# Two transformer blocks on one core: the norms between the layers taken tile by tile, and their scale vectors moved into the weights

## The chip, the cores and the metric

The kernel runs on one core of a Trainium2 chip. The metric is the device time of one execution in microseconds (us); lower is better. TensorE (PE) does the matrix products, VectorE (DVE), ScalarE (ACT) and GpSimd (POOL) the rest, and SyncE (SP) starts most of the loads. Each engine works through a queue of its own in order; engines are tied by semaphores.

## The reference, cut to what matters

Two blocks run over 512 tokens of width 1024, in float32. The part that matters here lies between the first block's mixer and the second block's input projection:

```
mix = concat(attention, gmlp) @ w_out                       # [512, 1024]
h   = h + rms_norm(mix, norm_mix_post)
t   = rms_norm(h, norm_ffn_pre)
ffn = (silu(t @ w_gate) * (t @ w_up)) @ w_down              # inner width 2816
h   = h + rms_norm(ffn, norm_ffn_post)
proj = rms_norm(h, attn_norm_2) @ w_in_2                    # [512, 2048], start of block 2
rms_norm(x, g) = x * rsqrt(mean(x*x) + 1e-6) * g
```

So behind each of the products with w_out and w_down there are two norms in a row: one of the product, whose result is added to the residual, and one of the sum, which feeds the next product. Block 2 goes on with attention, a pooling mixer, routing over 32 experts, and the experts; none of that is touched.

## The kernel before, in words

Tokens lie in four tiles of 128. X holds the residual, four tiles of [128, 1024]. XP is the input of a projection, transposed (features on partitions, 8 feature tiles by 512 tokens), as a high and a low part; each product is made of three matmuls, high by high, high by low, low by high (pe_mm3, lines 225 to 228).

The weights come in chunks of at most 4 feature tiles by 512 columns (front_chunks, line 58; w_out is chunks 14 to 17, w_gate_up 18 to 39 in 11 pairs, w_down 40 to 51, w_in_2 52 to 59). SP loads them, by a list in order, into three ring slots (sp_load). ScalarE copies a loaded chunk into WH (act_split, line 214) and VectorE makes the remainder WL (dve_split, line 222). There are three slots of WH and WL, so the split of one chunk waits for the end of the product three splits before (semaphore p_pr), and the product waits for w_lo. A split's number is four below its chunk's number here: split 13 is chunk 17. A chunk of w_out, w_down or w_in_2 has four outputs, one for each token tile, in PSUM banks 0 to 3 (H0) or 4 to 7 (H1); a chunk of w_gate_up has four outputs of 128 features by 512 tokens.

Behind w_out and behind w_down stands the same pair of norms. act_post squares the eight outputs (line 351) and, once X is updated, X's four tiles (line 357). dve_post adds the sums (line 361), has POOL take the power -0.5 of all four columns (line 282), and then for each tile and half scales the product out of PSUM (line 373) and adds it to X (line 376). When all four tiles are there, the mean (line 277), the power and four diagonal tiles (line 287) are made, and pe_rms_T multiplies X by the diagonals, which scales and transposes at once (line 300; a float32 matmul leaves two records). act_put and dve_put (lines 310 and 317) scale by norm_ffn_pre or attn_norm_2 on the way from PSUM into XP. Both vectors lie transposed in GT, columns 8 to 15 and 16 to 23.

The ffn runs in eleven steps f of 256 gate and 256 up columns: two splits, then silu on ScalarE (line 1107) and the product with up on VectorE (line 1129), which writes HIDT. For w_down, HIDT is copied and split four feature tiles at a time, into two buffers in turn (HID2, lines 1085 and 1091); the last block has two tiles. The first copy waits for all of f = 10. The order on each engine is written out by hand in act_wout, dve_wout, act_ffn, dve_ffn, act_mix2 and dve_mix2. act_mix2 issues eleven loads on ScalarE's queue (lines 1204 to 1208) and then small steps for the rotary tables, which VectorE shares (lines 1271 to 1300).

Of the kernel before, what the change touches and what calls it, by code (L numbers as in the profile page):

```python
# [7 lines left out]
F32 = mybir.dt.float32  # L8
# [16 lines left out]
H0, H1 = (0, 1, 2, 3), (4, 5, 6, 7)  # L25

# [20 lines left out]
class Chunk:  # L47
# [4 lines left out]
    def __init__(self, src, k0, nk, cols, nout, raw=False):  # L52
        self.src, self.k0, self.nk, self.cols = src, k0, nk, cols
        self.w = sum(w for _, w in cols)
        self.nout, self.raw = nout, raw


def front_chunks():
# [3 lines left out]
    def columns(src, cols, nout, nk=8):  # L62
        for k0 in range(0, nk, 4):
            out.append(Chunk(src, k0, 4, cols, nout))

    def both(src, nk):
        for k0 in range(0, nk, 4):
            for half in range(2):
                out.append(Chunk(src, k0, min(4, nk - k0), [(512 * half, 512)], 4))
# [9 lines left out]
    both("w_out", 8)  # L79
# [5 lines left out]
    both("w_out_2", 8)  # L85
# [25 lines left out]
def program(nc, A):  # L111
    ctx = ExitStack()
    with ctx:
# [46 lines left out]
        SSN = SMALL[:, 28:32]  # L160
        XP = (RA[:, 0:4096].rearrange("p (k n) -> p k n", k=8), RA[:, 4096:8192].rearrange("p (k n) -> p k n", k=8))
        HID2 = [tuple(RA[:, 4096 * z + 2048 * c:4096 * z + 2048 * c + 2048].rearrange("p (k n) -> p k n", k=4) for c in range(2))
# [43 lines left out]
        def act_split(e, j):  # L206
# [7 lines left out]
            e.activation(WH[:, j % 3, 0:n], RING[:, ch.slot, 0:n], ACT.Copy).then_inc(s("w_hi"), 1)  # L214

        def dve_split(e, j):
            if j not in SPLIT:
# [4 lines left out]
            e.tensor_tensor(WL[:, j % 3, 0:n], RING[:, ch.slot, 0:n], WH[:, j % 3, 0:n].bitcast(F32), ALU.subtract  # L222
                            ).then_inc(s("w_lo"), 1)
# [45 lines left out]
        POW = {"mix": 1, "gln": 2, "post1": 3, "ffn": 4, "post2": 5, "mix2": 6, "moe": 7, "emb": 11, "gate": 12}  # L269
        XT = {"mix": 0, "mid": 8, "ffn": 16, "mix2": 24, "qk": 32, "mid2": 40, "emb": 48, "gate": 50}  # L270
        DG = {"mix": 1, "ffn": 2, "mix2": 3, "gate": 4}
# [72 lines left out]
        def act_post(e, p, c, JUNK, junk2):  # L344
            for half in range(2):
                for i in range(4):
                    n = 8 * p + 4 * half + i
                    e.wait_ge(s("p_pr"), CH[c[half]].first_out + i + 1)
                    if n:
                        e.wait_ge(s("a_sp"), n)  # L350
                    e.activation(JUNK[:, 0:512], PS[(H0, H1)[half][i]][:, :], ACT.Square,
                                 accum_out=SSP[:, 4 * half + i:4 * half + i + 1]).then_inc(s("a_sp"), 1)
            for i in range(4):
                e.wait_ge(s("v_x"), 8 * p + 2 * i + 2)
                if i >= 2:
                    e.wait_ge(s("a_ss"), 4 * (p + 1) + i - 1)
                e.activation(junk2[i % 2], X[:, i, :], ACT.Square, accum_out=SSN[:, i:i + 1]).then_inc(s("a_ss"), 1)

        def dve_post(e, p, stage, GROW, JUNK, row):
            e.wait_ge(s("a_sp"), 8 * p + 8)  # L360
            e.tensor_tensor(SS4, SSP[:, 0:4], SSP[:, 4:8], ALU.add).then_inc(v_c.sem, v_c.up())
            e.wait_ge(v_c.sem, v_c.n)
            dve_mean(e, stage, SS4, 1.0 / 1024, EPS)
            e.wait_ge(s("g_r4"), POW[stage])
            e.wait_ge(s("d_row"), row)
            for i in range(4):
                for half in range(2):
                    b = (H0, H1)[half][i]
# [2141 lines left out]
```

## Time and profile before

| | us |
|---|---|
| median of 3 runs (2344.99 to 2345.92) | 2345.06 |
| the profiled execution's own time | 2344.97 |
| its span | 2343.0 |
| TensorE busy | 2144.6 (92%) |
| VectorE busy | 1542.5 (66%) |
| ScalarE busy | 1338.4 (57%) |
| GpSimd busy | 263.2 (11%) |

The span is the stretch between the first and the last recorded instruction; the execution's own time has about 2 us around it. A busy engine is one with an instruction running; PEclk is the clock that was granted to TensorE, 1.00 for 2.4 GHz and 0.50 for 1.2 GHz. Durations of matmuls contain the way through the array, so the cost of one in a stream is the distance from start to start.

### The profile page before, as it was taken

Reading aid. Unit: us, or ns where it says so; the run is one execution under the profiler, and the core shown is the slowest. Engines: PE = TensorE matmul, PEld = TensorE weight load, DVE = VectorE, ACT = ScalarE, POOL = GpSimd, SP = SyncE. Lnnn points to the kernel's source line nnn. Section 1 sums busy time; section 2 is a strip of 40 time slices with the busy share of each in tenths; the row PEclk is TensorE's granted clock in tenths of the full one; section 3 lists DMA queues with packets and bytes.
Section 4 is the critical chain, followed back from the end, with each engine's and each line's share of the span. In section 5 each row is a group of like instructions: output and inputs, shape, how many; then the busy total and the mean of one; then the engine's idle time right before and its main releaser. Section 6 shows DMA issues by size and latency. Waiting matters only on the chain.

```text
span 2343.0 us, 31680 instructions
## 1 busy us (share of the span) xinstructions
PE 2144.6 (92%) x10622; PEld 1769.4 (76%) x10622; DVE 1542.5 (66%) x1777; ACT 1338.4 (57%) x1690; POOL 263.2 (11%) x254
## 2 busy tenths in 40 slices
PE   3985798699989879886999999999999999999999
PEld 3874687588868767665788888888888888888877
DVE  3214782422223245657898898898988988988884
ACT  3212452312222233423788888888888888888874
POOL 0000000000000000002221221211222212212220
PEclk9987699799999989798999999999999999999999
DMA  3332001122322312032899999999999999999971
GB/s 136 95 125 80 1 2 63 50 103 90 106 74 81 116 65 95 1 115 82 329 366 372 359 369 362 364 364 360 373 365 361 374 358 373 357 361 367 370 278 66
DMA packets 87455, 511.25 MB, mean 218 GB/s; under 512 B 17286, under 2 KB 19930, under 8 KB 29787
## 3 DMA queue, kind: packets, MB, share of 16 engines
q1 hardware_dynamic: 70304, 484.46, 55.1%
q0 software_dynamic: 9536, 16.81, 2.9%
q10 hardware_dynamic: 7546, 9.06, 1.2%
q8 instruction: 45, 0.74, 0.1%
q14 instruction: 24, 0.19, 0.0%
HBM read 503.44 MB, written 23.07 MB: 225 GB/s over the span
## 4 chain that ended last, share of the span: by engine, by line
PE 88%; DVE 6%; ACT 2%; issue 2%; DMA 2%; ACTq 1%; POOL 0%; POOLq 0%; DVEq 0%; SPq 0%
PE PS L1995 15%; PE PS L1997 15%; PE PS L1996 15%; PE PS L226 10%; PE PS L227 10%; PE PS L228 10%; PE PS L1992 2%; PE PS L907 1%; PE PS L300 1%; PE PS L1885 1%; PE PS L2005 1%; DMA RING<-c_oh 1%; PE PS L975 1%; PE PS L1335 1%; PE PS L552 1%
## 5 line engine op out<-in xcount | busy, mean ns | idle before, releaser
L1879 DVE TENSOR_TENSOR WL<-RING,WH 128x2048 fp32r<-128x2048 f32 x388 | 879.6, 2287 | 95.3 <-ACT WH L1875 92.0
L1875 ACT ACTIVATE WH<-RING 128x1024 fp32r<-128x1024 f32 x776 | 811.7, 1059 | 200.2 <-PE PS L1997 176.9
L1995 PE MATMUL PS<-WH,RA 128*128 128x512 f32 x1540 | 639.5, 415 | 0.0
L1997 PE MATMUL PS<-WH,RA 128*128 128x512 f32 x1540 | 600.9, 390 | 0.0
L1996 PE MATMUL PS<-WL,RA 128*128 128x512 f32 x1540 | 600.4, 390 | 0.0
L222 DVE TENSOR_TENSOR WL<-RING,WH 128x2048 fp32r<-128x2048 f32 (+2 forms) x60 | 133.5, 2224 | 482.4 <-ACT WH L214 482.4
L214 ACT ACTIVATE WH<-RING 128x2048 fp32r<-128x2048 f32 (+2 forms) x60 | 111.6, 1860 | 478.0 <-PE PS L228 446.8
L1997 PEld LDWEIGHTS PS<-WH,RA 128*128 128x128 f32 x1540 | 289.5, 188 | 62.8
L1996 PEld LDWEIGHTS PS<-WL,RA 128*128 128x128 f32 x1540 | 290.2, 188 | 59.0
L1995 PEld LDWEIGHTS PS<-WH,RA 128*128 128x128 f32 x1540 | 291.2, 189 | 54.5
L226 PE MATMUL PS<-WH,RA 128*128 128x512 f32 (+2 forms) x640 | 246.7, 385 | 18.8 <-DVE RA L1091 10.0
L227 PE MATMUL PS<-WL,RA 128*128 128x512 f32 (+2 forms) x640 | 245.2, 383 | 0.0
L228 PE MATMUL PS<-WH,RA 128*128 128x512 f32 (+2 forms) x640 | 244.8, 383 | 0.0
L226 PE MATMUL PS<-RA,WH 128*128 128x512 f32 x416 | 162.4, 390 | 0.3 <-ACT AR L598 0.3
L228 PE MATMUL PS<-RA,WL 128*128 128x512 f32 x416 | 161.9, 389 | 0.0
L227 PE MATMUL PS<-RA,WH 128*128 128x512 f32 x416 | 161.9, 389 | 0.0
L226 PEld LDWEIGHTS PS<-WH,RA 128*128 128x128 f32 x640 | 122.8, 192 | 43.0 <-issue 11.1
L228 PEld LDWEIGHTS PS<-WH,RA 128*128 128x128 f32 x640 | 122.5, 191 | 23.5
L227 PEld LDWEIGHTS PS<-WL,RA 128*128 128x128 f32 x640 | 122.7, 192 | 22.8
L2161 POOL DMA_INDIRECT acc_scr<-AR,SMALL x32 | 69.8, 2182 | 331.6 <-issue 331.6
L282 POOL TENSOR_TENSOR SMALL<-SMALL 128x4 f32<-128x4 f32 x8 | 9.0, 1122 | 853.4 <-DVE SMALL L277 853.4
L930 ACT ACTIVATE AR<-AR 128x128 f32<-128x128 f32 (+3 forms) x96 | 53.9, 562 | 78.3 <-DVE AR L949 77.2
(346 smaller groups left out, 2269.8 us busy)
## 6 DMA issues: line engine op xcount, KB each, us to landing
RING<-w_experts SPq DMA_DIRECT2D x390, 1024.0 KB, 7.2
RING<-w_front SPq DMA_DIRECT2D x60, 1024.0 KB, 4.9
X<-x SPq DMA_DIRECT2D x4, 512.0 KB, 5.8
acc_scr<-X SPq DMA_DIRECT2D x4, 512.0 KB, 3.5
xs_scr<-AR ACTq DMA_DIRECT2D x4, 512.0 KB, 3.1
X<-acc_scr SPq DMA_DIRECT2D x4, 512.0 KB, 5.2
out<-X SPq DMA_DIRECT2D x8, 256.0 KB, 2.0
AR<-AR ACTq DMA_DIRECT2D x12, 128.0 KB, 4.2
```

What stands on the lines that cost most here:

```text
L214: e.activation(WH[:, j % 3, 0:n], RING[:, ch.slot, 0:n], ACT.Copy).then_inc(s("w_hi"), 1)
L222: e.tensor_tensor(WL[:, j % 3, 0:n], RING[:, ch.slot, 0:n], WH[:, j % 3, 0:n].bitcast(F32), ALU.subtract).then_inc(s("w_lo"), 1)
L226: e.matmul(out, a[0], b[0], start=start, stop=False)
L227: e.matmul(out, a[0], b[1], start=False, stop=False)
L228: return e.matmul(out, a[1], b[0], start=False, stop=stop)
L930: e.activation(PX[z][:, 0:w], LG[z][:, 0:w], ACT.Exp, bias=NM[:, z:z + 1], scale=-1.0, accum_out=RS[:, n:n + 1]).then_inc(s("a_ex"), 1)
L1875: e.activation(WH[:, m % 3, v], RING[:, m % 6, v], ACT.Copy).then_inc(s("m_hi"), 1)
L1879: e.tensor_tensor(WL[:, m % 3, :], RING[:, m % 6, :], WH[:, m % 3, :].bitcast(F32), ALU.subtract).then_inc(s("m_lo"), 1)
L1995: e.matmul(PS[bank][:, :], lhs[0][:, kr + k, :], WH[:, m % 3, c], start=False, stop=False)
L1996: e.matmul(PS[bank][:, :], lhs[0][:, kr + k, :], WL[:, m % 3, c], start=False, stop=False)
L1997: x = e.matmul(PS[bank][:, :], lhs[1][:, kr + k, :], WH[:, m % 3, c], start=False, stop=(stop and k == 3))
L2161: e.indirect_dma_start(acc_d, bass.IndirectOffsetOnAxis(TCOL, 0), YY, None, bounds_check=511, oob_is_err=False, compute_op=ALU.add).then_i ...
```

## The change

- act_post, dve_post, the diagonal tiles and the scaled transposes between the layers go. In their place act_joint, dve_joint, pool_joint and pe_joint_T do both norms for one token tile after another, in an interleaved order. The squares of the half-0 outputs, and their product with the post norm's vector, are taken while the half-1 chunk is still being multiplied. The sum goes into X in one 1024 wide instruction for each tile. ScalarE scales the updated row (a_xr), TensorE transposes it plainly, and high and low parts are written for one token tile at a time.
- norm_ffn_pre and attn_norm_2 are multiplied into the weights during the splits of w_gate_up and w_in_2 (four pieces of 512 columns, each with its own column of GT).
- The first ffn columns (f = 0) are multiplied for tokens 0 to 255 first and for tokens 256 to 511 after that, as products 256 columns wide. The first chunk of w_in_2 is taken token tile by token tile.
- The w_down rows are cut as 2, 4, 4, 4, 4, 4 tiles instead of 4, 4, 4, 4, 4, 2; the first hidden copy moves ahead of the last two silus and waits only for chunk 38.
- The chunk behind each pair of norms (splits 16 and 50) is split after the norms; the loads of act_mix2 are issued behind that.

```diff
+DOWN_ROWS = ((0, 2), (2, 4), (6, 4), (10, 4), (14, 4), (18, 4))
...
     for f in range(11):
-        columns("w_gate_up", [(256 * f, 256), (FF + 256 * f, 256)], 4)
-    both("w_down", 22)
+        columns("w_gate_up", [(256 * f, 256), (FF + 256 * f, 256)], 4, gain=8)
+    both("w_down", DOWN_ROWS)
     for grp in (0, 1, 3, 2):
-        columns("w_in_2", [(grp * 512, 512)], 4)
+        columns("w_in_2", [(grp * 512, 512)], 4, gain=16)
...
-            e.activation(WH[:, j % 3, 0:n], RING[:, ch.slot, 0:n], ACT.Copy).then_inc(s("w_hi"), 1)
+            if ch.gain is None:
+                x = e.activation(WH[:, j % 3, 0:n], RING[:, ch.slot, 0:n], ACT.Copy)
+            else:
+                for k in range(ch.nk):
+                    v = slice(ch.w * k, ch.w * k + ch.w)
+                    g = ch.gain + ch.k0 + k
+                    x = e.activation(WH[:, j % 3, v], RING[:, ch.slot, v], ACT.Copy, scale=GT[:, g:g + 1])
+            x.then_inc(s("w_hi"), 1)
...
+                    x = e.scalar_tensor_tensor(WL[:, j % 3, v], RING[:, ch.slot, v], GT[:, g:g + 1], WH[:, j % 3, v].bitcast(F32),
+                                               ALU.mult, ALU.subtract)
...
+        def pool_joint(e, p):
+            for kind, i in JORD:
+                m, r = ((M4, R4), (MX4, RX4))[kind == "X"]
+                e.wait_ge(s("v_m4"), jpow(p, kind, i))
+                e.tensor_tensor(r[:, i:i + 1], m[:, i:i + 1], NEGH[:, 0:1], ALU.pow).then_inc(s("g_r4"), 1)
...
+            def sums(i):
+                e.wait_ge(s("v_x"), 8 * p + 2 * i + 2)
+                if i:
+                    e.wait_ge(s("a_ss"), 4 * (p + 1) + i)
+                e.activation(JX, X[:, i, :], ACT.Square, accum_out=SSN[:, i:i + 1]).then_inc(s("a_ss"), 1)
+
+            def rows(i):
+                e.wait_ge(s("g_r4"), jpow(p, "X", i))
+                e.activation(XR[i], X[:, i, :], ACT.Copy, scale=RX4[:, i:i + 1]).then_inc(s("a_xr"), 1)
+
+            def high(i):
+                for half in range(2):
+                    e.wait_ge(s("p_xt"), XT[stage] + 2 * i + half + 1)
+                    e.activation(XP[0][:, 4 * half:4 * half + 4, 128 * i:128 * i + 128],
+                                 PS[TBK[p][i][half]][:, :].rearrange("p (k n) -> p k n", k=4), ACT.Copy).then_inc(s("a_xt"), 1)
...
+            (ACT)  out0 out1 sums0 out2 rows0 sums1 out3 high0 rows1 sums2 high1 rows2 sums3 high2 rows3 high3
+            (DVE)  out0 add0 out1 mean0 add1 out2 mean1 add2 out3 low0 mean2 add3 low1 mean3 low2 low3
...
+            def out(i):
+                e.wait_ge(s("a_sp"), 8 * p + 4 + i + 1)
+                e.tensor_scalar(M4[:, i:i + 1], SSP[:, i:i + 1], SSP[:, 4 + i:5 + i], 1.0 / 1024, ALU.add, ALU.mult
+                                ).then_inc(v_c.sem, v_c.up())
+                e.wait_ge(v_c.sem, v_c.n)
+                e.tensor_scalar(M4[:, i:i + 1], M4[:, i:i + 1], EPS, None, ALU.add).then_inc(s("v_m4"), 1)
+                dve_out_gain(e, p, c, 1, i, GROW)
+
+            def add(i):
+                e.wait_ge(s("g_r4"), jpow(p, "P", i))
+                e.wait_ge(v_c.sem, v_c.n)
+                e.scalar_tensor_tensor(X[:, i, :], JJ[i], R4[:, i:i + 1], X[:, i, :], ALU.mult, ALU.add).then_inc(s("v_x"), 2)
...
         def pe_ffn(e):
-            pe_rms_T(e, "ffn", DIAG2, {0: [("v_x", 8)]})
-            xt = xt_of("ffn")
+            pe_joint_T(e, 0, "ffn", 0, XR1)
+            pe_joint_T(e, 0, "ffn", 1, XR1)
+            w = [...]
+            for n, (bank, c0) in enumerate(((0, 0), (2, 256), (1, 128), (3, 384))):
+                if n == 0:
+                    e.wait_ge(s("v_xt"), XT["ffn"] + 4)
+                if bank >= 2:
+                    e.wait_ge(s("v_x"), 2 * bank + 2)
+                for k in range(8):
+                    pe_mm3(e, PS[bank][:, 0:256], tuple(v[:, k % 4, c0:c0 + 128] for v in w[k // 4]), tuple(v[:, k, 0:256] for v in XP),
+                           k == 0, k == 7)
+                if n < 2:
+                    pe_joint_T(e, 0, "ffn", 2 + n, XR1)
+            e.wait_ge(s("v_xt"), XT["ffn"] + 8)
+            (then the same for tokens 256 to 511, first k 0 to 3 of all four banks, then k 4 to 7, with p_pr)
...
         def pe_mix2(e):
-            pe_rms_T(e, "mix2", DIAG3, {0: [("v_x", 16)]})
+            pe_joint_T(e, 1, "mix2", 0, XR2)
+            pe_joint_T(e, 1, "mix2", 1, XR2)
+            for i in range(4):
+                e.wait_ge(s("v_xt"), XT["mix2"] + 2 * i + 2)
+                (12 matmuls of chunk 52 for token tile i)
+                if i < 2:
+                    pe_joint_T(e, 1, "mix2", 2 + i, XR2)
```

The lines in brackets stand for longer code of the diff. ScalarE's queue around the second pair is: split 49, four squares of half 0, the joint norms, split 50, the loads of act_mix2. Around the first pair it is: splits 13 and 14, four squares of half 0, split 15, the joint norms, split 16. SP's list of the routing stage gets one more wait, for the last square of X (a_ss).

## Rows read from the trace of the kernel before

**Rows 1.** The page, part 1: engine, busy us, share of the span, instructions.

```profile
PE 2144.6 (92%) x10622; PEld 1769.4 (76%) x10622; DVE 1542.5 (66%) x1777; ACT 1338.4 (57%) x1690; POOL 263.2 (11%) x254
```

**Rows 2.** Waits of PE, 350 to 950 us: who for whom, us, times, longest.

```profile
PE PS L300 <- DVE AR L287: 48.6, 2, 24.3
PE PS L226 <- DVE RA L1091: 10.0, 1, 10.0
```

**Rows 3.** Timeline at the first norm: start, us, instruction, idle before and releaser.

```profile
395.34 1.92 ACT L214 ACTIVATE WH<-RING 128x2048 fp32r<-128x2048 f32 x1 [8.96 <-PE PS L228]
...
406.22 1.91 ACT L214 ACTIVATE WH<-RING 128x2048 fp32r<-128x2048 f32 x1 [8.96 <-PE PS L228]
...
430.44 9.71 PE L300 MATMUL PS<-AR,X 128*128 128x128 f32 x64 [24.32 <-DVE AR L287]
...
462.05 1.92 ACT L214 ACTIVATE WH<-RING 128x2048 fp32r<-128x2048 f32 x1 [8.96 <-PE PS L228]
```

**Rows 4.** Timeline at the second norm.

```profile
811.99 1.91 ACT L214 ACTIVATE WH<-RING 128x2048 fp32r<-128x2048 f32 x1 [3.52 <-PE PS L228]
...
832.75 0.34 ACTq L1204 DMA_DIRECT2D RING<-c_mask  x1
...
851.24 0.19 DVE L1298 TENSOR_TENSOR AR<-AR 128x32 f32<-128x32 f32 x1 [0.41 <-ACT AR L1216]
...
857.13 1.92 ACT L214 ACTIVATE WH<-RING 128x2048 fp32r<-128x2048 f32 x1 [5.93 <-PE PS L228]
```

**Rows 5.** Timeline between the last gate and up columns and the down product.

```profile
679.65 1.91 ACT L214 ACTIVATE WH<-RING 128x2048 fp32r<-128x2048 f32 x1 [8.96 <-PE PS L228]
...
683.80 1.28 DVE L1129 TENSOR_TENSOR AR<-PS,AR 128x512 f32<-128x512 f32 x2
...
689.55 0.77 PE L226 MATMUL PS<-WH,RA 128*128 128x512 f32 x1 [10.00 <-DVE RA L1091]
```

**Rows 6.** Windows: stretch, length, each engine's busy us, granted clock, DMA share, GB/s.

```profile
410.00:415.00 5.00, 0.00 (x0) 0.00 (x0) 0.79 (x3) 3.71 (x12) 0.29 (x1) 0.64 0.60 211
...
434.00:436.00 2.00, 2.00 (x15) 2.00 (x14) 0.84 (x2) 0.96 (x2) 0.00 (x0) 0.68 0.00 0
...
961.00:971.00 10.00, 10.00 (x38) 7.86 (x38) 5.92 (x28) 3.71 (x14) 0.00 (x0) 0.50 0.00 0
```

**Rows 7.** Groups by shape, 361 to 1110 us: busy us, mean ns, idle before.

```profile
L222 DVE TENSOR_TENSOR WL<-RING,WH 128x2048 fp32r<-128x2048 f32 x45 | 103.1, 2292 | 347.8 <-ACT WH L214 347.8
...
L214 ACT ACTIVATE WH<-RING 128x2048 fp32r<-128x2048 f32 x45 | 86.2, 1915 | 368.4 <-PE PS L228 368.4
L310 ACT ACTIVATE RA<-PS,GT 128x512 fp32r<-128x512 f32 x20 | 13.8, 688 | 30.9 <-PE PS L1402 16.2 <-PE PS L300 14.7
L351 ACT ACTIVATE AR<-PS 128x512 f32<-128x512 f32 x16 | 9.5, 595 | 1.3
...
L1657 ACT ACTIVATE AR<-X,SMALL 128x1024 f32<-128x1024 f32 x4 | 4.6, 1150 | 3.4 <-POOL SMALL L1850 3.4
...
L1653 ACT ACTIVATE AR<-X 128x1024 f32<-128x1024 f32 x4 | 4.2, 1058 | 0.9 <-DVE X L1728 0.9
L351 ACT ACTIVATION_READ_ACCUMULATOR AR<-PS 128x1 f32 x16 | 3.1, 194 | 0.0
```

**Rows 8.** Timeline of the routing stage, one norm tile by tile.

```profile
1073.42 0.15 DVE L1732 TENSOR_SCALAR SMALL<-SMALL 128x1 f32<-128x1 f32 x1 [1.22 <-ACT AR L1653]
...
1073.65 0.55 POOL L1850 TENSOR_TENSOR SMALL<-SMALL 128x1 f32<-128x1 f32 x1 [238.41 <-DVE SMALL L1732]
...
1079.32 1.09 ACT L1646 ACTIVATE AR<-PS 128x512 f32<-128x512 f32 x2 [2.19 <-PE PS L1553]
```

**Rows 9.** Timeline of PE: narrow products, then eight transposes.

```profile
279.89 0.28 PE L970 MATMUL PS<-RA 128*128 128x256 f32 x1
280.01 0.27 PE L907 MATMUL PS<-CST,AR 128*128 128x128 f32 x1
...
1078.65 1.07 PE L1553 MATMUL PS<-CST,X 128*128 128x128 f32 x8
```

More of the change, by code:

```diff
@@ new lines, in dve_out_gain, with dve_joint, out, mean @@
+        def dve_out_gain(e, p, c, half, i, GROW):
+            e.wait_ge(s("a_sp"), 8 * p + 4 * half + i + 1)
+            e.tensor_tensor(JJ[i][:, 512 * half:512 * half + 512], PS[(H0, H1)[half][i]][:, :], GROW[:, 512 * half:512 * half + 512],
+                            ALU.mult).then_inc(v_c.sem, v_c.up())
+        def dve_joint(e, p, c, stage, GROW):
+            def out(i):
+                e.wait_ge(s("a_sp"), 8 * p + 4 + i + 1)
[8 more added lines that the diff above has]
+                e.scalar_tensor_tensor(X[:, i, :], JJ[i], R4[:, i:i + 1], X[:, i, :], ALU.mult, ALU.add).then_inc(s("v_x"), 2)
+            def mean(i):
+                e.wait_ge(s("a_ss"), 4 * (p + 1) + i + 1)
+                e.tensor_scalar(MX4[:, i:i + 1], SSN[:, i:i + 1], 1.0 / 1024, EPS, ALU.mult, ALU.add).then_inc(s("v_m4"), 1)
+            def low(i):
+                for half in range(2):
+                    v = (slice(None), slice(4 * half, 4 * half + 4), slice(128 * i, 128 * i + 128))
+                    e.wait_ge(s("a_xt"), XT[stage] + 2 * i + half + 1)
+                    e.tensor_tensor(XP[1][v], PS[TBK[p][i][half]][:, :].rearrange("p (k n) -> p k n", k=4), XP[0][v].bitcast(F32),
+                                    ALU.subtract).then_inc(s("v_xt"), 1)
+            out(0)
+            add(0)
+            out(1)
+            mean(0)
+            add(1)
+            out(2)
+            mean(1)
+            add(2)
+            out(3)
+            low(0)
+            mean(2)
+            add(3)
+            low(1)
+            mean(3)
+            low(2)
+            low(3)
@@ L380, in program, with pe_joint_T @@
+        def pe_joint_T(e, p, stage, i, XR):
+            e.wait_ge(s("a_xr"), 4 * p + i + 1)
+            if p == 0 and i == 2:
+                e.wait_ge(s("v_xt"), XT[stage] + 4)
+            for half in range(2):
+                for j in range(4):
+                    x = e.transpose(PS[TBK[p][i][half]][:, j * 128:(j + 1) * 128], XR[i][:, (4 * half + j) * 128:(4 * half + j + 1) * 128], IDT)
+                x.then_inc(s("p_xt"), 1)
         GR = ar(0, 128, 0, 84)
@@ L1028, in act_wout @@
             e.dma_start(ROWS, A["norm_mix_post"].broadcast_to([128, 1024])).then_inc(s("d_row"), 16)
[L1029 to L1031 removed]
+            act_split(e, 13)
+            act_split(e, 14)
+            for i in range(4):
+                act_out_squares(e, 0, (16, 17), 0, i)
+            act_split(e, 15)
+            act_joint(e, 0, (16, 17), "ffn", XR1)
+            act_split(e, 16)
         def dve_wout(e):
@@ L1062, in pe_ffn @@
                 free = {}
-                if f == 0:
-                    free = {n: [("v_xt", XT["ffn"] + 5 + n)] for n in range(4)}
                 if f >= 2:
```

233 lines of the change are left out of this document (126 added, 107 removed).

## The prediction, made before the changed kernel ran

> **What bounds the kernel now.** The page's first part comes first: TensorE is busy 92% of the span, far ahead of VectorE and ScalarE [rows 1]. So time can be had only where TensorE stands still, runs at half clock, or is given less to do. TensorE's waits over the stretch from the output projection to the second layer's input projection [rows 2] name three such places: two waits of 24.3 us each for the diagonal tiles of line 287 (the norms between the layers), and one of 10.0 us for line 1091 (the first hidden tiles of the down product). They are 58.6 of the 2343 us.
>
> The timeline of the first norm [rows 3] shows the whole price. The split that starts at 406.22 is released by the last w_out product; call that moment E. The split at 462.05 is released by the end of the first ffn columns (chunks 18 and 19). Two chunks of products are 2 x 10.88 us (395.34 to 406.22 is one), so of these 55.8 us 21.8 are products and 34 are norm: 24.3 of idle time and 9.7 of scaled transposes, one long record of 64 instructions. For the second norm [rows 4] the same reading gives 857.13 - 811.99 = 45.1 us from E to the end of chunk 52, again 34 of norm over 10.9 of products. In the middle place [rows 5], chunk 39 is done at 679.65 and the down product starts at 689.55, after a split, the last two silus and products, and a 2048 wide copy and subtraction of hidden tiles.
>
> The granted clock [rows 6] is 0.64 over 410 to 415 and 0.68 over 434 to 436. It fell to 1.2 GHz some 5 us after TensorE stopped, and was back at 2.4 GHz some 5 us after it had started again at 430.44. The norm therefore also costs about 5 us at half clock, in the transposes.
>
> **The change, part by part. Durations.** The row groups by shape [rows 7] and two timelines [rows 8, 9] of stages that do such things already hold nearly every new operation. On ScalarE a 512 square out of PSUM takes 0.60 and its accumulator 0.19: 0.78. A 1024 square takes 1.06 and 0.19: 1.25. Scaling a 1024 row takes 1.15. A pair of 512 copies out of PSUM takes 1.09, so the second adds 0.5. On VectorE two 512 operations on PSUM take 1.28 [rows 5], 0.64 each. The new 1024 wide multiply-add is not in the trace; half of the 2048 subtraction is 1.15, and the fixed part on top makes 1.27, which I take. A tile's mean takes 0.15, the pow on POOL starts 0.08 after it and takes 0.55 [rows 8]. A transpose takes 1.07/8, about 0.11 behind others, and twice that at half clock.
>
> **Weights scaled in the splits.** 30 chunks (22 of w_gate_up, 8 of w_in_2) are now split in four pieces of 512. ScalarE pays 4 x 0.69 at most (2.45 with overlap) instead of 1.92, VectorE 2.75 instead of 2.29, so a split is ready 1.0 us later. Three slots let a split start when the chunk three back is done, 21.8 us before it is needed, and it takes 5.2. I cost it at nothing; without that cover it would be 30 x 1.0 us.
>
> **First norm.** Times are from E, each engine in its queue's order. ScalarE squares the last half-0 output at -10.8, then splits chunk 19 (-10.1 to -7.6). VectorE's part of that split ends at -4.8. Then tile 0: two tiny sums 0.4, pow 0.65, add 1.27, so X's first tile is ready at -2.5. From here ScalarE is never free: square of X0 1.25, square of output 2 0.78, scale row 0 1.15, square X1 1.25, output 3 0.78, two copies 1.04, row 1 1.15, square X2 1.25, which ends at 6.25. VectorE, held by that last sum, does mean 0.2, add of tile 3 1.27 and the two low parts of tile 1, 1.28: 9.05. That opens the half-token products at E + 9.1; before, products began at about E + 34. From there TensorE is the limit. All 192 products of 256 columns take 192 x 0.12 = 23.0 us (line 970's, 279.89 to 280.01 [rows 9]). The transposes of tiles 2 and 3, placed between them, take 1.8. Half clock lasts until some 5.1 us after the start, so 2.5 are lost. The end is E + 36.4, where before it was E + 55.8: 19 us less (19.1 unrounded). Tile 3's row is ready at 17.4 and wanted at 18.3, its low parts at 20.8 and wanted at 25.0. Chunk 20's split, now behind the whole norm in both queues, is ready at 25.3 and wanted at 36.4; behind it the load of chunk 23 moves from 410 to about 431, more than three chunks ahead of its use.
>
> The unseen 256 column stream of three products with a new weight each is bounded by the transposes' 0.11 from below and by the 512 columns' 0.227 from above. The nearest row gives 0.12, and I keep 0.11 to 0.18 for the range: 1.9 us less, or 11.5 more.
>
> The Trainium skill (TensorE: Matmul & The Clock Gate, Back-to-back issue gap) has N/2.4 + 2.5 ns between products at full clock, 109 ns at 256 columns and 216 at 512. By that estimate the split into token halves would cost 0.2 us, where the rows' 0.12 and 0.227 give 1.3. The rows decide.
>
> **Transition to the down product.** The first block of rows becomes two tiles instead of four, and its copy is put ahead of the last silus. ScalarE: split 679.65 to 681.5, hidden copy of 1024 1.06, two silus to 683.6. VectorE: split to 683.9, low part 1.15 (half of 2.29), then the two products of line 1129, 1.28: 686.3. TensorE starts there instead of at 689.55: 3.2 us. What is late next is the last gate product, not the hidden tiles; the second block has some 11 us of products in front of it. The clock falls and recovers as before.
>
> **Second norm.** Here chunk 53's split stands ahead of the half-0 squares, so VectorE begins tile 0 only at E - 3.0 (split to -5.6, four gains 2.6), and X0 is ready at -0.7. ScalarE's chain gives row 1 at 6.8, the two tiles' transposes at half clock end at 8.6, and tile 0's low parts are ready at 7.6. So products run from 8.6: 48 x 0.227 = 10.9, transposes 1.8, half clock 1.7: E + 23.0. Before it was 45.1, so 22 us less. Behind it ScalarE issues its eleven loads and the rotary setup, now only after chunk 54's split, from E + 20.8. In the trace this takes 851.24 - 832.75 = 18.5 us, most of it waiting for the norm; even at its full length chunk 55 is split by E + 44.5, and TensorE wants it at 44.7. No cost, but little margin by that upper bound. SP's new wait (a_ss) is for an event long past when it gets there. The rest of the program is anchored to TensorE's progress and moves as a block.
>
> **Sum.** 19.1 + 3.2 + 22.0 = 44.3 us off the profiled execution's own 2344.97 (span 2343.0), 2300.7; the median is 0.09 higher: 2301.
>
> **The rivals.**
> *The helpers are slower than their rows* (strided writes, hand-offs of 0.1, semaphores between three engines). For: the chain to the first product is some twenty steps in three queues, and a hand-off too many shifts all behind it. Against: each step has a measured twin. With every ScalarE, VectorE and POOL step 15% longer the two norms give 16.2 + 19.4, total 38.8: 2306. With 30%, 30.0 + 3.2: 2312.
> *The clock stays low between the bursts.* For: over 961 to 971 TensorE has work in every microsecond and is granted 0.50 [rows 6]; here it gets 1.0 and 1.8 us of transposes with waits around them before the products. Against: once the products start nothing in my chain lets TensorE stand. One more 5 us at half clock in each of the three places costs 2.5 each: 2308.5. Were the clock never to fall, 2.5, 2.7 and 2.5 us come back: about 2293.
> The Trainium skill (TensorE: Matmul & The Clock Gate, HAM oscillation — how this bites in real kernels) describes short bursts of products between waits that fall back to half clock each time; what that would do here is the 2308.5 above.
> *Half-width products cost like wide ones.* At 0.18 us, 11.5 us come back: 2312.
> *The overlap is not there.* If queue order made each tile run its full chain of some 7.5 us before the next, two tiles would be ready at about E + 11.4 and all four at E + 26, which the products on the first half mostly cover; 3 to 5 us lost: 2305. It ends inside the first rival's range.
> *Slower than before: the split weights arrive late.* The pieces wait on a [128,1] operand each. From 2.7 us a piece on either engine ((10.88 - 0.64)/4, rounded up) a chunk's splitting outlasts its products, and TensorE waits in all 30 chunks. At 3.2 us a piece it is 30 x 2.6 = 77 us: 2345 - 44 + 77 = 2378. Line 310 does the same operation in 0.69, so it would have to be wrong four times over.
>
> **How the numbers follow.** Forecast, 2293 to 2306: 0.72. Helpers 15 to 30% slower or the low clock, 2306 to 2313: 0.16, and half-width cost 0.05. Late split weights 0.02, something unforeseen beside it 0.05. What this measurement can't tell from no change is 0.2%, 4.7 us. To reach it 40 of the 44 us would have to go: 0.02. Faster 0.95, slower 0.03. The range runs from the never-falling clock, 2293, to a little beyond the 30% case, 2315.
>
> **What would show it.** Chunk 17's end to chunk 19's end near 36 us, instead of 55.8; chunk 51's end to chunk 52's near 23, instead of 45.1; TensorE's gap before the down product near 7, instead of 10. The 256 column products start 0.12 us apart at full clock. ScalarE, not VectorE, is without gaps from E - 2.5 to E + 6. No idle time of TensorE on line 226 within the ffn columns; if there is, the scaled splits are late and the forecast is wrong. It is wrong too if the first half-token product starts after E + 15, or if the stretch behind chunk 52 shows a wait for split 51.

## The result and the profile after

| | before | after |
|---|---|---|
| median of 4 runs each | 2345.49 us | 2325.68 us |
| the single runs | 2344.99, 2345.06, 2345.92, 2363.85 | 2321.04, 2324.92, 2326.44, 2326.5 |
| the profiled execution's own time, span | 2344.97, 2343.0 | 2321.04, 2319.2 |
| mean granted clock of TensorE in it | 0.953 | 0.951 |

The ratio is 0.989, with a 95% interval of 0.984 to 0.994. That is a gain of 20 us, under 1%, and not of 44, and the time is outside the forecast range of 2293 to 2315. The fourth run of before, 18 us above the other three, is the first sign of the explanation.

The first part of the page after, beside [rows 1], and the granted clock in 40 slices of 58 us:

```profile
PE 2158.7 (93%) x10654; PEld 1781.9 (77%) x10654; DVE 1553.7 (67%) x1869; ACT 1361.8 (59%) x1788; POOL 272.0 (12%) x266
PEclk9987699999999997597999999999999999999999
```

The same line of before:

```profile
PEclk9987699799999989798999999999999999999999
```

TensorE is recorded busy 14 us longer although it does nearly the same products. In the line of before the 7 in the eighth slice and the 8 in the fifteenth are the two norms; both have gone. But in the slice that starts at 928 us after shows 5 where before shows 7. That stretch is the second block's attention, which the change doesn't touch.

TensorE's waits of after from 350 to 950 us, beside [rows 2]: who for whom, us, times, longest.

```profile
PE PS L476 <- ACT AR L397: 11.1, 4, 3.5
...
PE PS L243 <- DVE AR L1261: 6.8, 1, 6.8
...
PE PS L243 <- DVE RA L449: 1.7, 1, 1.7
```

The two waits of 24.3 us for the diagonal tiles have become four for scaled rows, 11.1 together, and one of 1.7 for the low parts; 10.0 us before the down product have become 6.8. No wait for a scaled split is in the list.

### The profile page after: what moved, and what is told of

Same layout as the page of the kernel before. It is cut to its first block, busy times and chain, and to the rows that moved or that the text cites. A ratio compares the mean times of both kernels' runs of the same rounds, so it can differ in the third digit from the quotient of the medians.

```text
span 2319.2 us, 31953 instructions
## 1 busy us (share of the span) xinstructions
PE 2158.7 (93%) x10654; PEld 1781.9 (77%) x10654; DVE 1553.7 (67%) x1869; ACT 1361.8 (59%) x1788; POOL 272.0 (12%) x266
## 3 DMA queue, kind: packets, MB, share of 16 engines
q1 hardware_dynamic: 70304, 484.46, 55.8%
## 4 chain that ended last, share of the span: by engine, by line
PE 88%; DVE 5%; DMA 2%; ACT 2%; issue 2%; ACTq 1%; POOL 0%; SPq 0%; DVEq 0%; POOLq 0%
PE PS L2130 15%; PE PS L2132 15%; PE PS L2131 15%; PE PS L243 10%; PE PS L244 10%; PE PS L245 10%; PE PS L2127 2%; PE PS L1010 2%; PE PS L2020 1%; PE PS L2140 1%; PE PS L1469 1%; DMA RING<-c_oh 1%; PE PS L1078 1%; PE PS L655 1%; DMA RING<-w_front 1%
## 5 line engine op out<-in xcount | busy, mean ns | idle before, releaser
L233 DVE TENSOR_TENSOR WL<-RING,WH 128x2048 fp32r<-128x2048 f32 (+2 forms) x30 | 64.7, 2156 | 236.6 <-ACT WH L218 236.6
L238 DVE SCALAR_TENSOR_TENSOR WL<-RING,GT,WH 128x512 fp32r<-128x512 f32 x120 | 82.1, 746 | 188.6 <-ACT WH L223 188.6
L218 ACT ACTIVATE WH<-RING 128x2048 fp32r<-128x2048 f32 (+2 forms) x30 | 54.2, 1805 | 227.1 <-PE PS L245 195.9
L223 ACT ACTIVATE WH<-RING,GT 128x512 fp32r<-128x512 f32 x120 | 76.8, 713 | 183.9 <-PE PS L245 183.9
L243 PE MATMUL PS<-RA,WH 128*128 128x512 f32 (+1 forms) x448 | 169.4, 378 | 2.0 <-DVE RA L449 1.7
L245 PE MATMUL PS<-RA,WL 128*128 128x512 f32 (+1 forms) x448 | 168.6, 376 | 0.0
L244 PE MATMUL PS<-RA,WH 128*128 128x512 f32 (+1 forms) x448 | 168.6, 376 | 0.0
```

Of the source, the lines that this page charges most:

```text
L218: x = e.activation(WH[:, j % 3, 0:n], RING[:, ch.slot, 0:n], ACT.Copy)
L223: x = e.activation(WH[:, j % 3, v], RING[:, ch.slot, v], ACT.Copy, scale=GT[:, g:g + 1])
L233: x = e.tensor_tensor(WL[:, j % 3, 0:n], RING[:, ch.slot, 0:n], WH[:, j % 3, 0:n].bitcast(F32), ALU.subtract)
L238: x = e.scalar_tensor_tensor(WL[:, j % 3, v], RING[:, ch.slot, v], GT[:, g:g + 1], WH[:, j % 3, v].bitcast(F32), ALU.mult, ALU.subtract)
L243: e.matmul(out, a[0], b[0], start=start, stop=False)
L244: e.matmul(out, a[0], b[1], start=False, stop=False)
```

## Where the time went, read from moments that both traces share

Every split on ScalarE that waits for TensorE marks the end of a chunk's products. These moments are compared below; after's are these rows of ScalarE's timeline (start, us, instruction, idle before and releaser), beside [rows 3 to 5]:

```profile
384.08 2.57 ACT L223 ACTIVATE WH<-RING,GT 128x512 fp32r<-128x512 f32 x4 [8.96 <-PE PS L245]
...
442.96 2.56 ACT L223 ACTIVATE WH<-RING,GT 128x512 fp32r<-128x512 f32 x4 [3.20 <-PE PS L245]
...
660.58 1.91 ACT L218 ACTIVATE WH<-RING 128x2048 fp32r<-128x2048 f32 x1 [9.82 <-PE PS L245]
...
777.90 2.56 ACT L223 ACTIVATE WH<-RING,GT 128x512 fp32r<-128x512 f32 x4 [8.31 <-PE PS L245]
...
833.75 2.56 ACT L223 ACTIVATE WH<-RING,GT 128x512 fp32r<-128x512 f32 x4 [6.37 <-PE PS L245]
...
888.15 1.91 ACT L218 ACTIVATE WH<-RING 128x2048 fp32r<-128x2048 f32 x1 [8.96 <-PE PS L245]
...
1046.04 0.60 ACT L1781 ACTIVATE AR<-PS 128x512 f32<-128x512 f32 x1 [1.15 <-PE PS L1688]
```

They are the ends of chunks 15, 19, 39, 50, 54 and 59 (59 is the last of the second input projection), and the first square of the routing norm. The last two have these twins in the trace of before:

```profile
933.29 1.91 ACT L214 ACTIVATE WH<-RING 128x2048 fp32r<-128x2048 f32 x1 [8.96 <-PE PS L228]
...
1070.78 0.60 ACT L1646 ACTIVATE AR<-PS 128x512 f32<-128x512 f32 x1 [1.15 <-PE PS L1553]
```

| stretch | before | after | gained | forecast |
|---|---|---|---|---|
| chunk 17's end (E; after: 384.08 + 2 x 10.88 = 405.84) to chunk 19's end | 55.8 | 37.1 | 18.7 | 19.1 |
| TensorE's gap before the down product | 9.9 | 6.7 | 3.2 | 3.2 |
| chunk 51's end (after: 777.90 + 10.88 = 788.78) to chunk 54's, two chunks behind 52 | 66.9 | 45.0 | 21.9 | 22.0 |
| chunk 59's end to the routing norm | 137.5 | 157.9 | -20.4 | 0 |

At chunk 59's end the changed kernel was 933.29 - 888.15 = 45.1 us ahead (forecast 44.3). The three rows add up to 43.8 of these. The rest is 406.22 - 405.84 = 0.4 us by which it was ahead at E already, and 0.9 us behind the start of the down product, where the clock was full again after 3.3 us instead of 5.2. At the routing norm it was 24.7 ahead: what is missing was lost in 158 us of unchanged code. Windows of after over the second block's attention (stretch, length, busy us of PE, PEld, DVE, ACT, POOL, granted clock, DMA share, GB/s):

```profile
906.00:916.00 10.00, 9.45 (x34) 7.48 (x34) 5.34 (x29) 3.84 (x17) 0.00 (x0) 0.50 0.00 0
916.00:936.00 20.00, 20.00 (x74) 16.02 (x73) 12.00 (x56) 6.27 (x22) 0.00 (x0) 0.50 0.01 2
936.00:956.00 20.00, 20.00 (x72) 15.68 (x71) 9.54 (x37) 5.27 (x15) 0.00 (x0) 0.50 0.00 0
956.00:976.00 20.00, 20.00 (x76) 15.42 (x75) 8.72 (x33) 5.89 (x15) 0.00 (x0) 0.55 0.01 1
```

TensorE is recorded busy in all of 916 to 976 us and runs at 1.2 GHz throughout, from 906.0 to 974.3, which is 68.3 us. In before the stretch of the same work begins low too [rows 6, last row], but the clock comes back after 20.5 us (950.7 to 971.2). After spent 47.8 us more at the low clock. If the 20.4 us lost are all of that stretch, its work took 27.4 us in before and ran 1.74 times as long in after; whether the clock alone makes such a ratio is seen below.

## The experiments

Three questions: is the course of the clock in the attention tied to the change? What decides it? Were the parts of the change worth what the forecast says, once the clock is out of the way? The kernels ran in four batches, each on one chip with runs of the kernel before beside them: a_pad2, b_pad13, a_fill and b_fill; a_again, a_best and b_best; a_rev, a_full0, a_hidlate and a_plainsplit; a_burst. The ratios set a kernel against whatever mixture of before's two times came up (the changed kernel itself has 0.989 above and 0.981 below), so the text compares groups of times. Where it sets a kernel of one batch beside one of another (a_rev, a_full0, a_hidlate and a_plainsplit beside a_best), a difference of 1 us in the times is not resolved: the medians of before's short and long runs differ by up to 1.4 and 0.8 us between batches. There the distances inside the traces decide. Names that begin with a_ build on the changed kernel, those with b_ on the kernel before.

### Shifting the moment: a_pad2, b_pad13

```diff
+                    if o == 0 and k == 0:
+                        for _ in range(again):
+                            e.matmul(out, a[0], b[0], start=True, stop=True)
...
-            pe_project(e, 56, full(H0), XP, 0, 8, free, {})
+            pe_project(e, 56, full(H0), XP, 0, 8, free, {}, again=2)
```

> The changed kernel with two products repeated (0.45 us of TensorE) at the start of chunk 56, ahead of the second block's attention; the repeats are overwritten, so the result is unchanged. Theory A (moment): the attention lost 20 us because its sparse products met the decisions on TensorE's clock 0.4 us earlier in their course than in the kernel before, and stayed at 1.2 GHz; with 0.45 us more they stand as in the kernel before, the low stretch in attention shrinks from 68 to about 20 us, and the profiled execution takes about 2301.5. Theory B (content): the attention is slower because of what the change left behind (order of queues, splits, placement); then the low stretch stays and the time is 2321 to 2326 plus 0.45.

> The kernel before with thirteen products repeated (2.95 us of TensorE) at the start of chunk 56; the result is unchanged. Theory A: its attention now stands against the clock's decisions as in the changed kernel, stays at 1.2 GHz for some 68 us and loses about 20 us: 2345 + 3 + 20 = 2368. Theory B: the attention of the kernel before is what it was, 2348.

a_pad2: 2304.5, 2306.02, 2306.62 and 2320.38 us. b_pad13 (again=13): seven runs of 2345.88 to 2347.33 and three of 2368.75 to 2372.78. The kernel before, beside them: nine runs of 2344.59 to 2347.05, sixteen of 2363.92 to 2368.76. So none of these kernels has one time: each has two, 14 to 27 us apart. In before the mean granted clock is 0.951 to 0.953 in the short runs and 0.942 to 0.945 in the long ones. Which one comes is not fixed by 0.45 or 3 us of shift, so the theory that the absolute moment decides fell: by it b_pad13 should always have had the longer time, and it had it three times in ten. Windows of a_pad2's profiled execution, one of its short ones:

```profile
916.00:936.00 20.00, 20.00 (x86) 15.97 (x85) 12.99 (x63) 6.93 (x25) 0.00 (x0) 0.61 0.01 2
936.00:956.00 20.00, 19.91 (x126) 15.45 (x125) 15.35 (x63) 9.71 (x27) 0.00 (x0) 1.00 0.01 1
```

The clock came back at 931.7 after 23.9 us low. Even so this short course cost more than the one in before's profile. From a_pad2's timeline:

```profile
889.75 1.91 ACT L218 ACTIVATE WH<-RING 128x2048 fp32r<-128x2048 f32 x1 [8.96 <-PE PS L245]
...
1030.89 0.60 ACT L1784 ACTIVATE AR<-PS 128x512 f32<-128x512 f32 x1 [1.16 <-PE PS L1691]
```

From chunk 59's end to the routing norm it took 141.1 us, where before took 137.5, and the clock was low for 40.9 us in three stretches of it (6.8, 23.9 and 10.2) where in before it was low for 34.1 (10.2, 20.5 and 3.4). These 3.6 us are most of the 5.3 by which this run, 2306.02, lies above the forecast's 2300.7. The attention works in 32 units, eight for each token tile. A unit of tile 0 spans one key tile (narrow), a unit of tile 3 four (wide), and it has a transpose for each of them. These transposes show the same work at either clock. After, then a_pad2 (PE's timeline; three transposes in a unit of token tile 2):

```profile
948.76 0.90 PE L1010 MATMUL PS<-CST,AR 128*128 128x128 f32 x3
952.13 0.90 PE L1010 MATMUL PS<-CST,AR 128*128 128x128 f32 x3
```

```profile
942.53 0.55 PE L1013 MATMUL PS<-CST,AR 128*128 128x128 f32 x3
944.39 0.55 PE L1013 MATMUL PS<-CST,AR 128*128 128x128 f32 x3
```

From start to start a unit takes 3.37 us at the low clock and 1.86 or 1.87 at the high one, 1.81 times as long: close to the 1.74 above, so the clock accounts for nearly all of the 20.4 us.

### The same kernel again: a_again

The kernel is the changed kernel, unedited.

> The changed kernel itself, once more, for the spread of its runs. The kernel before has now shown two groups, near 2345 (mean granted clock 0.953) and near 2366 (0.943), from one and the same program. Theory A' (two courses of the clock in the second block's attention, in any kernel; what kernel it is only shifts the chances): this one has two groups as well, near 2301 to 2306 at a mean clock of about 0.957 and near 2321 to 2327 at 0.947 to 0.951, each 40 to 44 us under its counterpart of before. Theory B' (the change's own effect is about 20 us and the groups of before are a separate matter): only one group, 2321 to 2327, in all runs.

Six runs: 2306.01, 2306.86, 2307.8 and 2320.67, 2320.98, 2322.74 us. The changed kernel has both times, as before has: beside it 6 of 17 runs of before lay at 2345.4 to 2347.0, 11 at 2364.9 to 2368.4. Of all 64 runs of before, with the first four, 20 were short and 44 long (2361.9 to 2368.8); of the changed kernel's 10 runs 3 were short. The profiled execution of a_again was a long one, and its attention was as after's: 68.3 us low, 157.95 us from chunk 59 to the routing norm. By the medians of these runs the change is worth 2346.2 - 2306.9 = 39.3 us short against short, and 2367.2 - 2321.0 = 46.2 long against long. Short and long don't have quite the same course in both kernels: with the 3.6 us read from a_pad2's trace above, the 39.3 become 42.9. For the 46.2 this can't be done, as there is no trace of a long run of before. The profile of before that the forecast was read from was a short run and after's a long one: that is the 20 us.

### Filling TensorE: a_fill, b_fill

```diff
+            def fill(e, u):
+                i, h, c = u
+                for _ in range((2, 1, 0, 0)[i]):
+                    e.matmul(PS[4][:, :], XP[0][:, h, i * 128:(i + 1) * 128], XP[0][:, 4 + h, :], start=True, stop=True)
```

(24 products, each behind the logits of a unit; nothing reads them.)

> The changed kernel with fill products in the second block's attention, into a bank that nobody reads: two of 512 columns for each unit of the first token tile, one for each unit of the second. Theory A: TensorE is busy enough to be given 2.4 GHz early and keep it; attention takes at most what it took in the kernel before, 2299 to 2303. Theory B: the attention is held by ScalarE and VectorE or by contention, the fill doesn't help: 2321 to 2330.

> The kernel before with the same fill. Theory A: little is left to win here, as the low stretch in attention was only 20 us: 2342 to 2347, and a_fill stays 43 to 45 us under it, which is the forecast for the change itself. Theory B: 2345 to 2350, and a_fill only about 20 us under it.

a_fill: ten runs of 2334.19 to 2337.28, ratio 0.992 (0.988 to 0.995). b_fill: ten of 2373.94 to 2377.21, ratio 1.007 (1.004 to 1.011). Windows of a_fill:

```profile
906.00:916.00 10.00, 9.38 (x30) 7.07 (x30) 3.31 (x18) 3.02 (x13) 0.00 (x0) 0.50 0.00 0
...
936.00:956.00 20.00, 20.00 (x69) 15.46 (x68) 9.19 (x38) 5.01 (x16) 0.00 (x0) 0.50 0.00 0
956.00:976.00 20.00, 20.00 (x72) 15.77 (x70) 8.92 (x36) 5.47 (x15) 0.00 (x0) 0.50 0.00 1
```

The theory that the engine merely has too little work in the narrow units was wrong. With more work between them the clock was low for 81.9 us in the profiled run (906.1 to 988.0), and all ten runs lie within 3.1 us of each other, above both of the changed kernel's groups. As a control the pair gives 2375.2 - 2335.8 = 39.4 us for the change. The courses are not quite alike: b_fill's clock was low for 75.1 us, and it took 167.3 us from chunk 59's end to the routing norm where a_fill took 170.3. With these 3.0 us the pair gives 42.4.

### Wide units first, and products in the waits: a_best, b_best

```diff
-        DIFF = [(i, h, c) for i in range(4) for h in range(4) for c in range(2)]
+        DIFF = [(i, h, c) for i in (3, 2, 1, 0) for h in range(4) for c in range(2)]
...
+            for _ in range(32):
+                e.matmul(PS[0][:, :], XP[0][:, 0, 0:128], XP[0][:, 1, :], start=True, stop=True)
```

The attention starts with token tile 3, whose units are four key tiles wide. 32, 12 and 8 products that nothing reads stand in three waits of TensorE: ahead of the rotary transposes, ahead of the attention and behind its second unit.

> The changed kernel with the second block's attention taken from the widest units to the narrowest (token tiles 3, 2, 1, 0) and with products that nobody reads where TensorE waits anyway: 32 of 512 columns in the 8.3 us wait for the rotary step, 12 behind the transposes, 8 behind the second unit's logits. Theory A': dense work up to the attention, and the dense units first, hold 2.4 GHz; all runs fall together, 2297 to 2304, at a mean clock over 0.955. Theory B' or a clock that doesn't follow dense work: the runs stay at 2321 or scatter over 20 us.

> The kernel before with the same order of attention units and the same idle-time products. Theory A': all runs together at 2341 to 2348, so that a_best less b_best gives the change alone: 41 to 45 us. Theory B': a_best is only about 20 us below.

a_best: 2294.49 to 2297.44, median 2296.62, ratio 0.974 (0.968 to 0.980). b_best: ten runs of 2338.97 to 2343.88, median 2340.84, ratio 0.992 (0.989 to 0.996). Windows of a_best:

```profile
906.00:916.00 10.00, 8.90 (x54) 6.42 (x53) 5.14 (x17) 5.57 (x13) 0.00 (x0) 1.00 0.00 0
916.00:936.00 20.00, 20.00 (x133) 16.12 (x132) 14.77 (x59) 8.70 (x23) 0.00 (x0) 1.00 0.01 2
936.00:956.00 20.00, 19.47 (x125) 15.53 (x124) 16.48 (x79) 9.89 (x35) 0.00 (x0) 1.00 0.00 1
956.00:976.00 20.00, 14.52 (x57) 11.35 (x56) 12.65 (x55) 4.76 (x14) 0.00 (x0) 0.66 0.00 0
```

The full clock is held through the wide units, and falls only among the narrow ones at the end. From chunk 59's end to the routing norm a_best takes 132.9 us and b_best 133.0, and the runs of each lie within 3 and 4.9 us. With the same time behind chunk 59 in both, **the change is worth 2340.84 - 2296.62 = 44.2 us; the forecast's sum was 44.3.** That they agree to 0.1 is luck: the two profiled runs are 41.9 us apart, and the pairs above gave 42.4 and 42.9. By these three the change is worth 42 to 44 us. a_best is also faster than both kernels of the case: 29 us below the median after.

### Which half of that edit does it: a_rev, a_burst

a_rev has only the order of the units, a_burst only the products in the waits.

> The changed kernel with the reversed order of attention units and no added products. If the order alone holds the clock: all runs 2296 to 2302. If the clock falls in the waits around the attention's start, the wide units begin at 1.2 GHz and may stay there: runs at 2320 or scattered.

> The changed kernel with the 32, 12 and 8 unread products of a_best in TensorE's three waits ahead of and inside the second block's attention, and its own order of units (tile 0 first). The theory that the order of units (the wide ones right behind the dense products) keeps the clock up expects that the products alone do little: two groups as in the changed kernel, near 2306 and 2321 us, with some 20 to 70 us at the low clock behind 905 us in the profile. The rival, that any full stretch of products just ahead is enough, expects one group near 2297 to 2302 with no low stretch in the attention.

a_rev: 2298.96 to 2302.8, median 2300.86, ratio 0.974 (0.969 to 0.979). a_burst: 2300.31 once and five runs of 2318.1 to 2319.81, ratio 0.979 (0.976 to 0.983). Windows of a_rev, then of a_burst:

```profile
906.00:916.00 10.00, 7.16 (x29) 5.45 (x30) 3.70 (x12) 4.10 (x8) 0.00 (x0) 0.66 0.00 0
916.00:936.00 20.00, 20.00 (x132) 15.95 (x131) 14.52 (x58) 8.92 (x23) 0.00 (x0) 1.00 0.01 2
```

```profile
896.00:906.00 10.00, 8.94 (x59) 7.43 (x58) 7.61 (x19) 4.03 (x8) 0.00 (x0) 1.00 0.00 0
906.00:916.00 10.00, 9.16 (x43) 6.95 (x42) 5.77 (x33) 5.12 (x18) 0.00 (x0) 0.81 0.00 0
916.00:936.00 20.00, 20.00 (x74) 15.75 (x73) 11.72 (x55) 6.27 (x22) 0.00 (x0) 0.50 0.01 2
```

The order does it. a_burst comes to the attention at the full clock, loses it at 912.4 for 61.4 us, and both groups of times are there again, 18 to 20 us apart, though with one short run of six. a_rev loses it early too, at 907.7, but has it back at 914.5, with the wide units. The products in the waits take another 4.2 us off by the medians. By the traces 2.2 of them lie between chunk 59's end and the routing norm, where a_rev takes 135.1 us and a_best 132.9.

### Single parts of the change: a_full0, a_hidlate, a_plainsplit

All three start from a_best, so that the clock blurs them less. a_full0 takes the first ffn columns on all tokens at once, a_hidlate puts the first hidden copy back behind the last silus and products, and a_plainsplit leaves the two scale vectors out of the splits, and so out of the result:

```diff
-            for n, (bank, c0) in enumerate(((0, 0), (2, 256), (1, 128), (3, 384))):
...
-            for f in range(1, 11):
+            pe_joint_T(e, 0, "ffn", 2, XR1)
+            pe_joint_T(e, 0, "ffn", 3, XR1)
+            for f in range(0, 11):
```

```diff
-                if f == 10:
-                    act_hidden(e, 0)
...
+            act_hidden(e, 0)
```

```diff
-        columns("w_gate_up", [(256 * f, 256), (FF + 256 * f, 256)], 4, gain=8)
+        columns("w_gate_up", [(256 * f, 256), (FF + 256 * f, 256)], 4)
```

> a_best with the first ffn columns on all 512 tokens at once, as in the kernel before, behind all four tiles' transposes. By the chain of queues (theory A': the change's own parts are priced by the rows): transposes run tile by tile, tile 3's low part is ready about 17.5 us after the last w_out product instead of the product starting at 9.3, and 21.8 us of products with 2.5 at half clock follow: end at E + 42, 5 us later than with token halves: 2302. A rival in which the half-width products waste what the early start gains: no difference, 2296.

> a_best with the first hidden copy and its low part behind the last two silus and products again, the two-tile first block kept. Theory A' as forecast: VectorE does the same three steps behind split 38 in another order, TensorE starts when the last of them is done, so nothing changes (within 0.3 us), and the 3.2 us of the transition come from the smaller block alone. Rival: the place of the copy matters, up to 1 to 2 us later.

> a_best with w_gate_up and w_in_2 split unscaled, one instruction of 2048 columns for each engine as in the kernel before; norm_ffn_pre and attn_norm_2 are left out of the computation. Theory A': 29 of 30 scaled splits are hidden; only splits 15 and 49, which stand in front of the norms' chains, come 1 us earlier each: 2294 to 2296.5. Rival (the scaled pieces slow the stream of chunks): 30 x 1.0 us less, 2270.

a_full0: 2300.6 to 2302.14, median 2301.49, ratio 0.974 (0.969 to 0.979). It is 4.9 us above a_best. From chunk 15's end to chunk 19's it takes 449.05 - 385.85 = 63.2 us, a_best 58.8; the half-token products are worth these 4.4.

a_hidlate: 2294.69 to 2296.01, median 2295.44: 1.2 us below a_best, where a difference of at most 0.3 was expected. The transition is as expected, though: TensorE waits 6.8 us ahead of the down product in both. So where the copy stands in the queue is worth nothing, and the transition's 3.2 us are left for the first hidden block being two tiles rather than four. No run has the change with a block of four.

a_plainsplit: 2329.14 to 2329.91, median 2329.57, 33 us above a_best, which looks like a refutation and is not. Without the vectors the routing gets other data, and there is more expert work, as a group of its trace shows (a_best has x1540 on that line):

```profile
L2139 PE MATMUL PS<-WH,RA 128*128 128x512 f32 x1588 | 659.4, 415 | 0.0
```

3 lines x 48 products x 0.227 us = 32.7 us, most of the 34.5 us that a_plainsplit takes longer behind the start of the routing norm. Up to the routing norm it is comparable: from chunk 15's end a_plainsplit takes 1019.92 - 385.67 = 634.25 us, a_best 1021.69 - 384.87 = 636.82. So the two are 2.6 us apart, where it would be 30 if the scaling weren't hidden. Of the 2.6 us 2.0 lie between chunk 15's end and chunk 19's. There a_plainsplit's first product stands 1.1 us earlier after the w_out products (E + 8.2 against E + 9.3), as split 15 alone would make it; the other 0.9 come with the clock, which is full again 3.9 us behind that product instead of 5.9. All that lies behind chunk 19's end makes 0.6.

## Why the prediction was wrong, and where it was right

**The failed step** is one sentence at the end of the second norm: "The rest of the program is anchored to TensorE's progress and moves as a block." Its instructions did; its clock did not. The sum has no term for the clock behind the second norm, where after lost 20.4 us. The step takes the course of the clock in the attention, of which [rows 6, last row] is a piece, as a property of the code. The experiments show it is one of two that the same program takes: the low stretch in the attention lasts 20 to 24 us in the traces of short runs (before, a_pad2) and 68 to 72 in those of long ones (after, a_again, b_pad13). The prediction even quoted that row, against the wrong stretch: it asked whether the new transposes would look like the attention to the clock, and never what else the attention itself could do.

**The range** followed from the same step. Three runs within 1 us of each other looked like a kernel with one time; 43 of the 60 later ones, beside the experiments, lay about 20 us higher. If the profiled time has a chance of one in three, the forecast has two likely values, 2301 and some 20 more. The range, ending at 2315, held none of the first four runs; the changed kernel's short runs, 2306 to 2308, lie within it, in its upper half.

**The three terms** were right: 18.7, 3.2 and 21.9 us against 19.1, 3.2 and 22.0. Their working has slips, of 0.3 us at most in the sum: 55.8 - 36.4 is 19.4 and not 19.1; the chain on ScalarE from -2.5 adds up to 6.15 and not 6.25; 1.07/8 is 0.13, though transposes do start some 0.11 apart; and 2.56 us a piece was rounded up to 2.7. The schedule inside the first norm came out nearly as written. Rows of after (start, us, instruction), E = 405.84:

```profile
403.18 1.06 ACT L393 ACTIVATE RING<-X 128x1024 f32<-128x1024 f32 x1 [2.15 <-DVE X L439]
...
411.44 1.97 PE L476 MATMUL PS<-CST,AR 128*128 128x128 f32 x8 [2.95 <-ACT AR L397]
...
415.10 0.58 PE L243 MATMUL PS<-RA,WH 128*128 128x256 f32 x1 [1.70 <-DVE RA L449]
...
421.80 0.29 PE L244 MATMUL PS<-RA,WH 128*128 128x256 f32 x1
...
421.92 0.28 PE L245 MATMUL PS<-RA,WL 128*128 128x256 f32 x1
```

X's first tile is there at E - 2.7 (forecast -2.5), the first half-token product starts at E + 9.3 (9.1), and at full clock the products stand 0.12 apart (0.12). The second norm's products start with the transposes of tile 1 just done, at 797.86, which is E + 9.1 (8.6). In the transition the down product is released at 667.25, 6.67 behind chunk 39's end.

**The scaled splits** were hidden, as forecast. Groups by shape from 345 to 1085 us, 30 splits in four pieces each:

```profile
L238 DVE SCALAR_TENSOR_TENSOR WL<-RING,GT,WH 128x512 fp32r<-128x512 f32 x120 | 82.1, 746 | 188.6 <-ACT WH L223 188.6
L223 ACT ACTIVATE WH<-RING,GT 128x512 fp32r<-128x512 f32 x120 | 76.8, 713 | 183.9 <-PE PS L245 183.9
```

A split takes 2.56 and 2.74 us, where 2.45 and 2.75 were forecast.

**A detail that was off.** ScalarE was to be free of gaps from E - 2.5 to E + 6. It had one of 0.31 us and one of 1.28, both for POOL:

```profile
404.60 2.09 POOL L375 TENSOR_TENSOR SMALL<-SMALL 128x1 f32<-128x1 f32 x2 [0.51 <-DVE SMALL L443]
...
406.19 1.15 ACT L397 ACTIVATE AR<-X,SMALL 128x1024 f32<-128x1024 f32 x1 [1.28 <-POOL SMALL L375]
...
412.56 1.28 DVE L439 SCALAR_TENSOR_TENSOR X<-RING,SMALL,X 128x1024 f32<-128x1024 f32 x1
...
412.68 1.56 POOL L375 TENSOR_TENSOR SMALL<-SMALL 128x1 f32<-128x1 f32 x1 [1.95 <-DVE SMALL L443]
...
416.73 0.54 POOL L375 TENSOR_TENSOR SMALL<-SMALL 128x1 f32<-128x1 f32 x1 [2.49 <-DVE SMALL L443]
```

The first product started 0.2 us later than forecast, so the cost was small. The power took 0.54 us alone, as in [rows 8], but 1.56 when it began beside VectorE's 1024 wide multiply-add, and ended 0.4 behind that one's end. The Trainium skill (GPSIMD Engine Reference, Key points) says that GpSimd shares its SBUF interfaces with VectorE and that instructions of VectorE with two SBUF inputs contend with it; the trace agrees, with 1 us on an instruction of one element per partition.

**The margin called small** held. The loads of act_mix2 went out from 806.63 (E + 17.9, forecast E + 20.8) to 811.34, beside and behind ScalarE's split of chunk 54, and VectorE waited for the last of them:

```profile
806.63 0.33 ACTq L1344 DMA_DIRECT2D RING<-c_mask  x1
...
811.34 0.53 ACTq L1348 DMA_DIRECT2D IDX<-positions  x1
...
817.92 0.22 DVE L1405 CUSTOM_DVE_ANT_0 AR<-RING 128x64 f32<-128x64 f32 x1 [5.60 <-DMA IDX<-positions]
...
821.41 5.00 ACT L223 ACTIVATE WH<-RING,GT 128x512 fp32r<-128x512 f32 x8
```

The last row is the splits of chunks 55 and 56 in one. Chunk 55's starts at E + 32.6, VectorE's part of it is done by E + 38, before the E + 44.7 at which TensorE wants it, and TensorE shows no wait for it.

**Still open:** what picks the course in a given execution. Two extra products came with three short runs of four, none with three of ten; by these counts that may be chance. The course just ahead doesn't tell it either: in after, a_again and a_pad2 the clock is low for 6.8 us and full for 6.8 us, and then low for 68.3, 68.3 and 23.9. In all kernels that have two times the narrow units are in front; the six kernels with the wide ones first showed no second time in 30 runs. But before has one trace, of a short run, and the changed kernel two, both of long runs, so a short and a long run of one program could not be set side by side.

## What to carry to other kernels

A low clock in a stretch that a change doesn't touch need not be a constant: look at the clock row for stretches below 1.00 that are neither idle nor short, and price what happens if they take another course before calling the rest a block. Where a profile is one execution, compare its mean granted clock and its time with several runs first; two groups of times mean two forecasts. To measure a change of 1 or 2%, put both kernels into a form in which that stretch has one course (here: widest units first), and check in the traces that it does take the same time in both; what is left is the change, here to within about 2 us.

## What the runs showed of the hardware that was not expected

- TensorE was at 1.2 GHz for 68.3 us with 67.75 of them recorded busy, and in the last 58.3 of these without a gap (after, 906.0 to 974.3). Here the busy share didn't tell the clock; the PEclk column has to be read by itself.
- One program, on one core, has two times 21 us apart (medians of before's 20 short and 44 long runs: 2345.6 and 2366.9). The Trainium skill (TensorE: Matmul & The Clock Gate, What's actually happening) calls the number of products at the low clock "run-variable" at a kernel's start and puts the cost below 1% of a typical span. The runs here agree that the clock's cost varies from run to run, by these 21 us, 0.9% of 2345. But here it sits in the middle of the kernel, and it hid half of the change's gain.
- With 24 products 512 columns wide added among the narrow ones the clock was low for 81.9 us. With the wide units first and nothing added (a_rev) it was low for 6.8 us in the first units and for 10.2 behind 962 us, with the same instructions in another order.
- Scaling in the split, by a column on each partition, costs ScalarE 0.64 us and VectorE 0.45 us per 128 x 2048 chunk (2.56 against 1.92, 2.74 against 2.29).
